# Dense units of a conformer step: the contraction outside, matmuls in turn on the unit's two output banks

## The reference, cut to what matters

```
h = rmsnorm(x);  z = h @ w_in      # 2048 -> GLU, q, k, v, indexer, gates
u = a * sigmoid(b);  conv = depthwise_causal(u, width 31)
c = silu(layernorm(conv)) @ w_conv_out
a = sparse_attention(q, k, v, indexer top-k) @ w_attn_out
x = x + (sigmoid(ga) * c + sigmoid(gb) * a) @ w_out
h = rmsnorm(x);  x = x + (silu(h @ w_gate) * (h @ w_up)) @ w_down   # 2048 -> 5632 -> 2048
y = rmsnorm(x)
```

## Time and profile before

| what | value |
|---|---|
| median of 3 runs | 2116.55 us (2115.48 to 2118.66) |
| profiled execution, its span from first to last instruction | 2114.4 us |
| instructions | 37,792, of them 14,113 matmuls and as many weight loads |
| TensorE busy | 2092.1 us (99%) |
| VectorE, ScalarE busy | 1088.5 us (51%), 835.5 us (40%) |
| DMA | 306.16 MB, mean 145 GB/s |

### The profile page before, as it was taken

One profiled execution on the slowest core, in us unless ns is written; L12 is line 12 of the kernel. 1 busy time (PEld: TensorE's weight loads), 2 busy tenths in 40 slices (PEclk: granted clock), 3 DMA queues, 4 the chain that ended last, 5 costly groups with the idle time before them and its releaser, 6 DMA issues.

```text
span 2114.4 us, 37792 instructions
## 1 busy us (share of the span) xinstructions
PE 2092.1 (99%) x14113; PEld 2051.3 (97%) x14113; DVE 1088.5 (51%) x1607; ACT 835.5 (40%) x1186; POOL 54.2 (3%) x78
## 2 busy tenths in 40 slices
PE   8999999999999999999999999999999999999997
PEld 6889999999999999999999999999999999999997
DVE  6456666766676533334555644444444333344454
ACT  5443344444445533334434433333333222233343
POOL 1000000000002000000000000000000000000000
PEclk9999999999999999999999999999999999999998
DMA  5345545444444445444444544544454444444443
GB/s 159 103 126 148 160 134 146 145 141 143 147 124 146 147 149 162 145 140 149 154 147 149 167 143 144 159 150 142 144 159 152 149 147 148 149 141 147 149 130 109
DMA packets 298362, 306.16 MB, mean 145 GB/s; under 512 B 12143, under 2 KB 294855, under 8 KB 298000
## 3 DMA queue, kind: packets, MB, share of 16 engines
q1 hardware_dynamic: 294672, 295.34, 45.8%
q0 software_dynamic: 3648, 10.25, 1.5%
HBM read 297.36 MB, written 8.19 MB: 145 GB/s over the span
## 4 chain that ended last, share of the span: by engine, by line
PE 98%; DVE 1%; DMA 0%; ACT 0%; issue 0%; SPq 0%; DVEq 0%; ACTq 0%
PE M L482 26%; PE M L484 26%; PE M L483 26%; PE T L484 5%; PE T L482 5%; PE T L483 5%; DMA x_tok<-in_x_sample 0%; PE S L625 0%; PE T L660 0%; PE T L634 0%; PE S L624 0%; PE S L790 0%; PE M L528 0%; PE T L665 0%; PE T L552 0%
## 5 line engine op out<-in xcount | busy, mean ns | idle before, releaser
L1160 DVE TENSOR_TENSOR w_lo<-w_raw,w_hi 128x1024 fp32r<-128x1024 f32 (+1 forms) x556 | 669.4, 1218 | 598.5 <-ACT w_hi L832 585.6
L832 ACT ACTIVATE w_hi<-w_raw 128x1024 fp32r<-128x1024 f32 (+1 forms) x556 | 574.3, 1051 | 558.7 <-PE M L484 380.5
L482 PE MATMUL M<-h_hi,w_hi 128*128 128x320 f32 (+1 forms) x1936 | 607.3, 314 | 0.2 <-DVE h_lo L1227 0.2
L483 PE MATMUL M<-h_lo,w_hi 128*128 128x320 f32 (+1 forms) x1936 | 598.6, 309 | 0.0
L484 PE MATMUL M<-h_hi,w_lo 128*128 128x320 f32 (+1 forms) x1936 | 598.6, 309 | 0.0
L482 PE MATMUL M<-o_hi,w_hi 128*128 128x320 f32 x1664 | 512.1, 308 | 0.0
L483 PE MATMUL M<-o_lo,w_hi 128*128 128x320 f32 x1664 | 511.7, 308 | 0.0
L484 PE MATMUL M<-o_hi,w_lo 128*128 128x320 f32 x1664 | 511.7, 308 | 0.0
L482 PEld LDWEIGHTS M<-h_hi,w_hi 128*128 128x128 f32 (+1 forms) x1936 | 363.1, 188 | 10.6 <-issue 6.6
L483 PEld LDWEIGHTS M<-h_lo,w_hi 128*128 128x128 f32 (+1 forms) x1936 | 363.3, 188 | 0.1
L484 PEld LDWEIGHTS M<-h_hi,w_lo 128*128 128x128 f32 (+1 forms) x1936 | 363.1, 188 | 0.1
(11 more groups left out here) (288 smaller groups left out, 1131.2 us busy)
## 6 DMA issues: line engine op xcount, KB each, us to landing
w_raw<-in_w_in SPq DMA_DIRECT2D x208, 512.0 KB, 3.7
w_raw<-in_w_gate SPq DMA_DIRECT2D x88, 512.0 KB, 4.3
w_raw<-in_w_up SPq DMA_DIRECT2D x88, 512.0 KB, 4.5
w_raw<-in_w_down SPq DMA_DIRECT2D x88, 512.0 KB, 3.4
w_raw<-in_w_attn_out SPq DMA_DIRECT2D x32, 512.0 KB, 4.7
w_raw<-in_w_out SPq DMA_DIRECT2D x32, 512.0 KB, 3.4
w_raw<-in_w_conv_out SPq DMA_DIRECT2D x16, 512.0 KB, 3.5
x_tok<-in_x_prompt SPq DMA_DIRECT2D x2, 1024.0 KB, 6.4
```

Source lines behind the costliest of these rows:

```text
L482: mm(out, w_hi[:, s, wc:wc + m], x_hi, start=start, stop=False)
L483: mm(out, w_hi[:, s, wc:wc + m], x_lo, start=False, stop=False)
L832: act_fn(w_hi[:, s, 0:n], w_raw[:, s, 0:n], ACT.Copy).then_inc(hi_ready, 1)
L1160: v.tensor_tensor(w_lo[:, s, 0:n], w_raw[:, s, 0:n], w_hi[:, s, 0:n].bitcast(f32), ALU.subtract)\
```

## The change: what it does

In `unit`, the loop over the contraction tiles goes outside and the loop over the two output tiles inside. The 24 matmuls then come in this order: high by high to bank 0, the same to bank 1, high by low to bank 0, to bank 1, low by high to bank 0, to bank 1, and so on for the next contraction tile. Both banks' `free` are waited for ahead of the first matmul. `units_used` is raised by the last matmul (to bank 1) and `first_done` by the one before it (to bank 0). Nothing else in the program changes.

```diff
                 tiles = [(b, b * P, min(P, n - b * P)) for b in range((n + P - 1) // P)]
-                for b, c, m in tiles:
-                    if first and free is not None:
+                if first and free is not None:
+                    for b, c, m in tiles:
 
                         pe.wait_ge(free[0], free[1](b))
-                    for kk in range(KU):
-                        wc = kk * n + c
-                        start, stop = first and kk == 0, last and kk == KU - 1
-                        x_hi, x_lo = hi[:, k0 + kk, :], lo[:, k0 + kk, :]
-                        out = banks[b][0:m, 0:T]
-                        mm(out, w_hi[:, s, wc:wc + m], x_hi, start=start, stop=False)
-                        mm(out, w_hi[:, s, wc:wc + m], x_lo, start=False, stop=False)
-                        done = mm(out, w_lo[:, s, wc:wc + m], x_hi, start=False, stop=stop)
-                    if b == len(tiles) - 1:
-                        done.then_inc(units_used, 1)
-                    elif last:
-                        done.then_inc(first_done, 1)
+                done = [None] * len(tiles)
+                for kk in range(KU):
+                    start, stop = first and kk == 0, last and kk == KU - 1
+                    x_hi, x_lo = hi[:, k0 + kk, :], lo[:, k0 + kk, :]
+                    for b, c, m in tiles:
+                        mm(banks[b][0:m, 0:T], w_hi[:, s, kk * n + c:kk * n + c + m], x_hi, start=start, stop=False)
+                    for b, c, m in tiles:
+                        mm(banks[b][0:m, 0:T], w_hi[:, s, kk * n + c:kk * n + c + m], x_lo, start=False, stop=False)
+                    for b, c, m in tiles:
+                        done[b] = mm(banks[b][0:m, 0:T], w_lo[:, s, kk * n + c:kk * n + c + m], x_hi, start=False,
+                                     stop=stop)
+                done[-1].then_inc(units_used, 1)
+                if last and len(tiles) == 2:
+                    done[0].then_inc(first_done, 1)
```

## The result

| | before | after |
|---|---|---|
| median, lowest to highest (us) | 2116.34 (2115.48 to 2118.66), 4 runs | 2144.22 (2142.73 to 2144.74), 4 runs |
| profiled execution, time and span | span 2114.4 | 2144.31, span 2142.8 |

The changed kernel is slower: ratio 1.0124, 95% interval 1.011 to 1.0139. It takes 27.9 us more by the medians, 28.4 by the two spans. The forecast was 2147.8, 31.2 more than the median then known, in a range of 2138 to 2158.

A forecast was written before the change was run, and what follows sets the result against it. TensorE, busy 99% of the span, was taken to bound the kernel. Pauses of 10.1, 0.2 and 20.6 us plus a 0.3 us tail, with 0 for the step, sum to 31.2: 2116.55 + 31.2 = 2147.8 us, range 2138 to 2158.

The forecast's parts named there:

- Part 1, the step: All unit matmuls: new order leaves the distance between matmul starts unchanged, 0 us, with 5.3 us to either side.
- Part 2, the places and their price: Group ends and starts: TensorE newly waits for emptyings where the next group uses the same two banks; 31.2 us with tail.
- The 27 places: Same-bank group starts: index-query passes 1 to 3, head passes 1 to 7, merge pass 0, 16 down-projection passes.
- behind ScalarE, each of 10: Head passes 1 to 7, merge pass 0, index passes 2 and 3: TensorE 1.01 us later each, 10.1 in all.
- behind VectorE, each of 16: Each of the 16 down-projection passes: TensorE's second matmul 1.29 us later, 20.6 us in all.
- tail, to the last sums: Kernel's end: last add to x comes 0.26 us later, and the square and last sums wait for it: 0.3 us.
- the way from the emptying's end to TensorE's weight load: At each pause: 0.11 us from the end of what TensorE waited for to its weight load.
- a down pass of 8 units takes 1.3 us longer: First down-projection: a sign that the forecast is right, each pass of 8 units lengthened by 1.3 us.
- (a): Every matmul: 13.4 ns wholly or partly a wait for the bank just written; faster, at most 177 us, 1971; 6%.
- (b): At the pauses: TensorE's clock falls to half, 1.8 us each, 47 us more, 2195; 4%.
- (c): At the pauses: hidden after all, change within noise; each would have to be under 0.16 us; 3%.
- (d): All unit matmuls: step grows a little under alternation; 0.4 ns gives 2153, inside the range; 10%.

The follow-up runs named there:

- e7: Kernel before, old order everywhere except one unit of each down-projection pass (fifth of eight, second of three), which alternates banks as in the change; 2110.58 us, ratio 0.9975.
- 256- and 128-column kernels: Kernel before and changed kernel, unit matmuls except each bank and group's first cut to 256 or 128 of 320 columns; only steps read: 118 and 112 ns.
- e1: Changed kernel, but each group's first and last unit keep the old order and waits; only units between alternate banks; 2113.27 us, ratio 0.999.
- e4: Changed kernel with odd down-projection passes on M2 and M3, even ones on T0 and T1, each waiting for the emptying two passes back; 2124.94 us, ratio 1.0043.
- e6: Kernel before, with banks alternating only in every second unit that is neither first nor last of its group; no wait moved; 2111.33 us, ratio 0.9978.
- e8: Kernel before, no alternation; in one unit of each down-projection pass each bank's four contraction tiles come in reverse; 2116.08 us, ratio 0.9998.

## Why the prediction was right

**What bounds the kernel.** The prediction had every new wait of TensorE count in full. It held: the shift between the traces grows at each pause, and only the shorter step of the down-projections takes some of it back. In the merge stage, with groups on other banks, it stays level.

**Part 1, the step.** A change of 0 was taken, with 5.3 us to either side. In the up-projections it is 0 (3,075 matmuls in 451 us both times). In the first down-projection the step went from 147.4 to 146.7, a gain of 0.14 us a pass, 1.1 there and some 0.4 in the second, inside the bound. That this was so small is in part luck: the prediction held that parting the two matmuls with the same weights loses nothing, and in e7's short state it is just this step that is 140 ns. The kernel before was in that state in none of its down-projection units; had it been, the turned order would have cost some 4.9 us more (an estimate: 2.3 ns for the 2,112 matmuls of the two down-projections). The Trainium skill (TensorE: Matmul & The Clock Gate, Back-to-back issue gap) gives N/2.4 + 2.5 ns as the gap of an isolated warm matmul, 135.8, 109.2 and 55.8 ns for 320, 256 and 128 columns. The rows have 146.7, 118 and 112, in both orders. The surplus is there but does not depend on the bank.

**Part 2, the places and their price.** The 27 places were the right ones: the waits name 26, and the 27th, index pass 1, had five transposes ahead and cost 0.14 us (0.2 forecast). The convolution and output groups and all merge groups but the first cost nothing, as said. The price was a little high:

| | forecast | measured |
|---|---|---|
| behind ScalarE, each of 10 | 1.01 | 0.97, merge pass 0 1.03 |
| behind VectorE, each of 16 | 1.29 | 1.19 to 1.22 at 13 places, 1.08 to 1.13 at pass 0 of each stage and pass 1 of the second |
| tail, to the last sums | 0.3 | 0.26 |

The term that was mis-sized is the way from the emptying's end to TensorE's weight load: 0.11 from a row near the end of the program, 0.05 at these places. The start of the emptying behind its matmul (0.35 and 0.46) and the pair's length (0.77 and 0.89) came within 0.02 of what the old rows gave. The lower prices take about 10 x 0.04 + 16 x 0.09 = 1.8 us off the 31.2, the step 1.5, and the longer start of that execution adds 0.7: 28.6, against 28.4 between the spans. The rest is the tail. The last sums start 0.26 later behind the last unit, as forecast, but the last of them starts only 0.01 later: at the end the granted clock falls to half, and in the changed kernel it falls further behind the sums' start (1.02 us against 0.75), so more of them run at full clock.

The sign "a down pass of 8 units takes 1.3 us longer" came as 1.08: the pause of 1.2 less the 0.14 of the step.

**The rivals.** (a) fell by the unchanged up-projections, by the 256- and 128-column kernels and by e1. (b), the clock, did not come: it reads 1.00 in the down-projection with its pauses. The Trainium skill (same page, A second HAM failure mode: psum-queue depth-cycling) tells of a kernel in which short idling between groups let the clock swing; the trace does not agree here, where 26 waits of 0.7 to 1.0 us left it at full. (c) fell by the 26 rows of waits. (d) did not come: the turned step is the same or shorter.

## What to carry to other kernels

The order inside an accumulation decides when its first bank can be emptied. If the next group needs the same bank, half a unit of matmuls is enough to hide the emptying, but only with both halves of the arrangement: bank 0 ends early, and each bank is waited for only where it is written. Going over all tiles at once cost nothing here where the groups change banks, so give such a loop a second pair of banks first (e4), or turn only in the units that are neither first nor last (e1). On a chain that is 98% one engine, such a pause can be priced to a tenth of a microsecond from rows of the old trace, but take the time that the engine needs to start again from a row where it starts into the same kind of work.

## What the runs showed of the hardware that was not expected

- The step of equal matmuls (128 x 128 weights, 320 columns, full clock) had three main values: 147.4, 146.7 and 144.4 ns. In old-ordered units on T0 and T1 it was the longest in the kernel before, and the shortest in e1, e6 and e7 behind the first turned one; it is a state of the stream that lasts. On M0 to M3 it was about 146.7 either way. This is worth 5.6 us in this kernel, and its cause is open.
- The step of matmuls with 128 columns was 112 ns at full clock, with 256 columns 118 (120 in the stages ahead of the up-projections). And the 128-column kernels did not keep the clock, though TensorE was busy for 98 to 99% of the time: from about 720 us on in the old order, and 745 in the turned one, it was at half to the end. TensorE's busy tenths and clock in 40 slices of the old-ordered one, and a stretch of its up-projections:

```profile
PE   8999999999999999999999999999999999999998
...
PEclk6555599998655555555555555555555555555555
```

```profile
1700.00:1800.00 100.00, 100.00 (x469) 100.00 (x468) 31.31 (x38) 23.86 (x30) 0.00 (x0) 0.50 0.33 100
```

- The half-clock stretch at the start varies in length. In the kernel before it was over by 28 to 32 us (0.98); in the profiled execution of e8, same start of the program:

```profile
28.00:32.00 4.00, 4.00 (x16) 2.65 (x14) 0.67 (x2) 1.06 (x2) 0.00 (x0) 0.50 0.48 131
```

Here 16 matmuls started where 25 did, and all units that follow are 5.5 us later in that execution (span 2118.8 against 2114.4). The median of its 11 runs is 2116.08, so a single trace should be compared stage by stage and not by its whole span.
